# Rotations by a shuffle on VectorE, and compression tokens split by ScalarE and VectorE in three buffers

## What is computed

```python
def rope(x, pos):
    half = ROT_DIM // 2                      # 16
    ...
    x1, x2 = xr[..., :half], xr[..., half:]
    rot = jnp.concatenate([x1 * cos - x2 * sin, x2 * cos + x1 * sin], axis=-1)

def compress(z, pe, w1, w2):                 # once for kc, once for vc
    zb = z[:, blk] + pe[None, None, :, None, :]      # 15 windows of 32 tokens, 16 apart
    zb = zb.transpose(0, 1, 3, 2, 4).reshape(b, n_cmp, NSA_KV_HEADS, CMP_LEN * HEAD_DIM)
    return jax.nn.silu(zb @ w1) @ w2

k_cmp = compress(k_c, cmp_pe[0], cmp_w1[0], cmp_w2[0])
v_cmp = compress(v_c, cmp_pe[1], cmp_w1[1], cmp_w2[1])
k_cmp = rope(k_cmp, positions[:, blk[:, -1]])
```

## Time and profile before

| | |
|---|---|
| median of 3 runs | 2145.42 us (2143.68 to 2145.71) |
| the profiled execution | 2145.21 us, its span 2143.4 us |
| TensorE busy | 2081.5 us, 97% of the span |
| VectorE busy | 1455.8 us, 68% |
| ScalarE busy | 996.9 us, 47% |
| GpSimd busy | 569.5 us, 27% |
| chain that ended last | TensorE 84%, GpSimd 6%, VectorE 5%, ScalarE 2% |
| `ks` to the end of `vw` with both compressions | 454.1 to 590.2 us of the span |

### The profile page before, as it was taken

How to read it: one execution, slowest core, us unless ns; L and a number is a source line. 1 busy time by engine, 2 the same in 40 slices (tenths; PEclk the granted TensorE clock), 3 DMA queues, 4 the chain that set the end, 5 groups by cost and what they waited for, 6 DMA issues and landing times.

```text
span 2143.4 us, 29511 instructions
## 1 busy us (share of the span) xinstructions
PE 2081.5 (97%) x11630; PEld 1770.5 (83%) x11630; DVE 1455.8 (68%) x1984; ACT 996.9 (47%) x1428; POOL 569.5 (27%) x551
## 2 busy tenths in 40 slices
PE   7999999999899999989999999999999999999997
PEld 6788888887788888778877888788888888888886
DVE  8866777677666556667655767677777557777755
ACT  5445444444532545443455554454454335454443
POOL 8205542233400244692121222311110001011122
PEclk9999999999999999999999999999999999999998
DMA  6554665555554433464544445555666665656664
GB/s 248 173 187 149 188 187 188 186 178 188 193 174 140 133 109 117 150 220 149 167 156 145 141 150 164 176 183 183 193 183 182 188 189 186 187 185 189 181 184 135
DMA packets 104090, 370.01 MB, mean 173 GB/s; under 512 B 11632, under 2 KB 12944, under 8 KB 103824
## 3 DMA queue, kind: packets, MB, share of 16 engines
q1 hardware_dynamic: 103952, 368.13, 54.5%
HBM read 365.98 MB, written 2.10 MB: 172 GB/s over the span
## 4 chain that ended last, share of the span: by engine, by line
PE 84%; POOL 6%; DVE 5%; issue 2%; ACT 2%; DMA 0%; SPq 0%; DVEq 0%; POOLq 0%; ACTq 0%
PE psg L508 46%; PE psg L510 22%; POOL s_zf L2357 2%; PE psg L555 2%; DVE s_wl L1579 2%; PE psg L557 2%; PE psg L556 2%; PE psg L507 2%; PE pst L508 1%; ACT s_wh L1064 1%; POOL s_acc L2533 1%; POOL s_psq L2526 1%; POOL s_psq L2281 1%; POOL s_acc L2284 1%; PE pst L592 1%
## 5 line engine op out<-in xcount | busy, mean ns | idle before, releaser
L1579 DVE TENSOR_TENSOR s_wl<-s_stage,s_wh 128x1024 fp32r<-128x1024 f32 (+3 forms) x699 | 869.4, 1245 | 391.8 <-ACT s_wh L1064 389.5
L1064 ACT ACTIVATE s_wh<-s_stage 128x1024 fp32r<-128x1024 f32 (+3 forms) x699 | 725.8, 1041 | 673.7 <-PE psg L508 360.2
L508 PE MATMUL psg<-s_ry,s_wh 128*128 128x512 f32 x2672 | 947.6, 402 | 3.4 <-DVE s_mv L1646 2.5
L510 PE MATMUL psg<-s_ry,s_wl 128*128 128x256 f32 x2501 | 705.0, 282 | 0.0
L508 PEld LDWEIGHTS psg<-s_ry,s_wh 128*128 128x128 f32 x2672 | 494.6, 189 | 121.0 <-issue 8.0
L508 PE MATMUL psg<-s_rh,s_wh 128*128 128x512 f32 x1280 | 462.5, 406 | 18.9 <-DVE s_rh L1597 9.1
L510 PEld LDWEIGHTS psg<-s_ry,s_wl 128*128 128x128 f32 x2501 | 474.4, 190 | 7.2
L510 PE MATMUL psg<-s_rh,s_wl 128*128 128x256 f32 x1180 | 333.0, 282 | 0.0
L508 PEld LDWEIGHTS psg<-s_rh,s_wh 128*128 128x128 f32 x1280 | 238.9, 189 | 78.7 <-issue 13.3
L508 PE MATMUL psg<-s_hid,s_wh 128*128 128x512 f32 x704 | 246.0, 399 | 0.0
L510 PEld LDWEIGHTS psg<-s_rh,s_wl 128*128 128x128 f32 x1180 | 225.1, 191 | 2.8
(11 more groups left out here) (389 smaller groups left out, 2318.2 us busy)
## 6 DMA issues: line engine op xcount, KB each, us to landing
s_stage<-in_wo SPq DMA_DIRECT2D x96, 512.0 KB, 3.6
s_stage<-in_wg SPq DMA_DIRECT2D x88, 512.0 KB, 3.5
s_stage<-in_wu SPq DMA_DIRECT2D x88, 512.0 KB, 3.9
s_stage<-in_ain SPq DMA_DIRECT2D x64, 512.0 KB, 3.5
s_stage<-in_wd SPq DMA_DIRECT2D x64, 448.0 KB, 3.4
s_stage<-in_wkv SPq DMA_DIRECT2D x32, 512.0 KB, 3.6
s_stage<-in_wd SPq DMA_DIRECT2D x32, 512.0 KB, 3.5
s_stage<-in_bq SPq DMA_DIRECT2D x24, 512.0 KB, 3.5
```

The costliest lines, as they stand in the source:

```text
L508: m = e.matmul(o, M.WH[:, r, ws], xx, start=begin, stop=end)
L510: m = e.matmul(o[:, T:2 * T], M.WL[:, r, ws], xh, start=False, stop=False)
L1064: e.activation(M.WH[:, c % NR, 0:n], M.ST[:, c % NS, 0:n], ACT.Copy).then_inc(S["wh"], 1)
L1579: e.tensor_tensor(M.WL[:, c % NR, 0:n], M.ST[:, c % NS, 0:n], M.WH[:, c % NR, 0:n], ALU.subtract).then_inc(S["wl"], 1)
```

## The change

The permutation product leaves TensorE. VectorE exchanges the halves itself with `stream_shuffle` from SBUF to SBUF; then, one tick later, sin and cos products follow in one tick, and one more tick later the sum. The rotation so takes as many ticks as before, has one VectorE instruction more, and no longer uses PSUM bank `o`.

In the compression GpSimd's part and the buffer `ZF` are gone. ScalarE reads the four strided token sets from `KC` or `VC` itself, with `pe` as its bias, and writes the high parts (four instructions in place of one); VectorE computes (Z + pe) - high over the same strided sets (four `scalar_tensor_tensor` in place of one `tensor_tensor`). `ZB` has three buffers, so step m may be written once TensorE has finished step m - 3.

```diff
@@ constants
-for _n, _w in (("ident", 128), ("cm", 128), ("ca", 32), ("c01", 32), ("ipool", 64), ("perm", 32),
+for _n, _w in (("ident", 128), ("cm", 128), ("ca", 32), ("c01", 32), ("ipool", 64),
...
-    put("perm", (a[:, None] == (a[None, :] + 16) % 32).astype(np.float32))
...
+HALVES = [(i + 16) % 32 for i in range(32)]
@@ Memory
-        self.ZF = alloc(l1c, "zf0", [128, 4, 128])
-        self.ZB = [alloc(l1c, f"zb{i}", [128, 2, 4, 128], F32R) for i in range(2)]
+        self.ZB = [alloc(l1c, f"zb{i}", [128, 2, 4, 128], F32R) for i in range(3)]
...
+    def zb(self, m, part, i):
+
+        return self.ZB[m % 3][:, part, i, :].rearrange("p (h n) -> p h n", h=4)[:, :, 0:15]
@@ tensor_program
-    def rope(r, x2, cols):
-        vacant(("o", r % 2))
-        w.wait_ge("l_con", 16)
-        e.matmul(M.PSO[r % 2][0:32, 0:cols], M.con("perm", 32, 32), x2, start=True, stop=True).then_inc(S["rp_mm"], 1)
-        held["o", r % 2] = ("rp_a", r + 1)
-
-    def rope_pair(r, dst, j, last):
-        yield
-        w.wait_ge(*last)
-        rope(r, dst[0:32, j - 1:j + 1, :], 512)
-
...
-                zb = M.ZB[m % 2]
+                zb = M.ZB[m % 3]
...
             if v == 0:
-                w.wait_ge("cmp", 1)
-                rope(3, M.KCMP[0:32, :, 0:15], 60)
                 yield
                 yield
...
             tile((n, j), H, ready("kv"))
-            if j % 2:
-                side.start(rope_pair((0, 1, 2, 4)[2 * r + j // 2], K, j, P.out[n, j]))
...
         tile(("q", j), Y, ready("h1"))
-        if j % 2:
-            side.start(rope_pair(5 + j // 2, M.QN, j, P.out["q", j]))
@@ scalar_program, compress
             def zb(m):
-                w.wait_ge("zf", 8 * v + m + 1)
-                if 8 * v + m >= 2:
-                    w.wait_ge("units", P.zb[8 * v + m - 2])
-                e.activation(M.ZB[m % 2][:, 0, :, :], M.ZF[:, :, :], ACT.Copy).then_inc(S["zbh"], 1)
+                Z = (M.KC, M.VC)[v]
+                w.wait_ge("zz", 3)
+                w.wait_ge(*P.out[("kc", "vc")[v], 3])
+                if m >= 3:
+                    w.wait_ge("units", P.zb[8 * v + m - 3])
+                elif v:
+                    w.wait_ge("units", P.zb[7])
+                for i in range(4):
+                    l = 4 * m + i
+                    x = e.activation(M.zb(m, 0, i), Z[:, :, l:l + 16 * 14 + 1:16], ACT.Identity, bias=M.vec("pe", 32 * v + l))
+                x.then_inc(S["zbh"], 1)
@@ vector_program
-    def rope(r, x2, cos, sin, n, wd, rt):
+    def rope(r, x2, cos, sin, n, wd, rt, made):
+
         rr = rt[:, :, :].rearrange("p a b -> p (a b)")[:, 0:n * wd].rearrange("p (a b) -> p a b", a=n)
-        w.wait_ge("rp_mm", r + 1)
+        w.wait_ge(*made)
         if r and r != 3:
             w.wait_ge("rp_c", 3 if r == 4 else r)
-        e.tensor_tensor(rr, M.PSO[r % 2][0:32, 0:n * wd].rearrange("p (a b) -> p a b", a=n), sin.unsqueeze(1).broadcast_to([32, n, wd]),
-                        ALU.mult).then_inc(S["rp_a"], 1)
-        yield
+        e.stream_shuffle(rr, x2, HALVES).then_inc(S["rp_s"], 1)
+        yield
+        w.wait_ge("rp_s", r + 1)
+        e.tensor_tensor(rr, rr, sin.unsqueeze(1).broadcast_to([32, n, wd]), ALU.mult).then_inc(S["rp_a"], 1)
         e.tensor_tensor(x2, x2, cos.unsqueeze(1).broadcast_to([32, n, wd]), ALU.mult).then_inc(S["rp_b"], 1)
         yield
...
                 w.wait_ge("zbh", 8 * v + m + 1)
-                e.tensor_tensor(M.ZB[m % 2][:, 1, :, :], M.ZF[:, :, :], M.ZB[m % 2][:, 0, :, :].bitcast(F32), ALU.subtract).then_inc(S["zbl"], 1)
+                Z = (M.KC, M.VC)[v]
+                for i in range(4):
+                    l = 4 * m + i
+                    x = e.scalar_tensor_tensor(M.zb(m, 1, i), Z[:, :, l:l + 16 * 14 + 1:16], M.vec("pe", 32 * v + l),
+                                               M.zb(m, 0, i).bitcast(F32), ALU.add, ALU.subtract)
+                x.then_inc(S["zbl"], 1)
@@ pool_program
-    def compress():
...
-    for i in range(2):
+    for i in range(3):
         e.memset(M.ZB[i][:, :, :, :].bitcast(F32), 0.0).then_inc(S["zz"], 1)
-    e.memset(M.ZF[:, :, :], 0.0).then_inc(S["zz"], 1)
-    side.start(compress())
```

More of the change, by code:

```diff
@@ L973, in tensor_program @@
     side.start(compress())
-    for r, (n, K) in enumerate((("ks", M.KS), ("kw", M.KW))):
+    for n in ("ks", "kw"):
         for j in range(4):
             tile((n, j), H, ready("kv"))
-            if j % 2:
-                side.start(rope_pair((0, 1, 2, 4)[2 * r + j // 2], K, j, P.out[n, j]))
     pair("vs", H, ready("kv"))
@@ L1850, in rope, with rope_pair @@
         e.tensor_tensor(x2, x2, rr, ALU.add).then_inc(S["rp_c"], 1)
-    def rope_pair(r, dst, j):
+    def rope_pair(r, dst, j, made):
         yield
-        yield from rope(r, dst[0:32, j - 1:j + 1, :], M.COS[:, :], M.SIN[:, :], 2, T, M.RT)
+        yield from rope(r, dst[0:32, j - 1:j + 1, :], M.COS[:, :], M.SIN[:, :], 2, T, M.RT, made)
     def compress():
@@ L1887, in compress @@
             if v == 0:
-                w.wait_ge("cmp", 1)
-                steps = rope(3, M.KCMP[0:32, :, 0:15], M.COS[:, 31:256:16], M.SIN[:, 31:256:16], 4, 15, M.RTC)
+                steps = rope(3, M.KCMP[0:32, :, 0:15], M.COS[:, 31:256:16], M.SIN[:, 31:256:16], 4, 15, M.RTC, ("cmp", 1))
                 next(steps)
@@ L2124, in vector_program @@
             if j % 2:
-                side.start(rope_pair((0, 1, 2, 4)[2 * r + j // 2], K, j))
+                side.start(rope_pair((0, 1, 2, 4)[2 * r + j // 2], K, j, P.out[n, j]))
     v_pair("vs", M.VS[:, 0, :], 1, "kv_c")
@@ L2136, in vector_program @@
         if j % 2:
-            side.start(rope_pair(5 + j // 2, M.QN, j))
+            side.start(rope_pair(5 + j // 2, M.QN, j, P.out["q", j]))
     w.wait_ge("hct", 2)
```

## The result

The changed kernel takes 2117.54 us, median of four runs (2116.44 to 2117.80), against 2145.19 of the kernel before on the same chip (four runs, 2143.68 to 2145.71): a ratio of 0.9868 with a 95% interval from 0.9856 to 0.9879. The forecast was 2118.3 us in a range from 2116 to 2129.

A forecast was written before the change was run, and what follows sets the result against it. TensorE, busy 97% of the span, was taken as the bound, idling in the compression stretches through GpSimd's loop. 11.6 + 1.2 + 8.45 + 6.62 - 1.0 = 26.9 us off 2145.2 gave 2118.3 us, range 2116 to 2129.

The forecast's parts named there:

- two products: Rotations: permutation products leave TensorE's path, 1.16 us each with refill; ten in all give 11.6 us.
- late splits: Both compression stretches: some weight splits come late on busy VectorE; 1.0 us given back for the 16 units together.
- The units as a measure: Both compression stretches: length beyond tile, value and compression unit times counts as lost, 8.45 us (keys) and 6.62 us (values).
- The loop: Compression: GpSimd's sums through one `ZF` hold up ScalarE's and VectorE's weight splits, hence TensorE; losses 8.45 and 6.62 us.
- z: Compression: VectorE's time for the four strided instructions of a step, taken as 0.85 us against 0.69 for the one.
- The first rival: Keys' stretch: VectorE becomes the bound if strided elements cost more; z = 2.0 gives 2125 us; chance 0.15.
- The shuffle: VectorE's eleven shuffles of 32 x 512: taken as 0.67 us each, beside TensorE's work, the wait at the scores staying covered.
- The compressed keys: After the product with `cmp_w2`: TensorE's wait for VectorE's copy and the permutation product go, 1.21 us.
- DMA: Both compression stretches: same bytes at about 225 GB/s, hidden until a load's landing takes over 6.2 us.
- The second: Compression stretches: staging slots become the bound, landings of 7 us costing 6 us, 2124 us; chance 0.10.
- the third: Compression stretches: the ring of weight splits, not GpSimd's loop, sets the pace; only 11.6 + 1.2 won, 2132 us; chance 0.07.
- The fourth: Compression: the strided instructions cost VectorE what they cost GpSimd, 4.36 us a step; slower, 2163 us; chance 0.03.

The follow-up runs named there:

- experiment 4: Kernel before with rotations by shuffles, the permutation's constant kept in place, GpSimd keeping the sums with two `ZF` and two `ZB`: 2125.1 us.
- experiment 10: Kernel before with rotations by shuffles, the permutation's constant kept in place, GpSimd keeping the sums with one `ZF` and three `ZB`: 2137.8 us.
- experiment 6: Changed kernel with two token buffers `ZB` in place of three: 2128.38 us.
- Experiment 12: Changed kernel with each of the eleven shuffles issued twice, the extra one into a buffer nothing reads at that time: 2117.65 us.
- experiment 3: Changed kernel with the 32 columns of the permutation's constant kept unused, so what lies behind stays in its place in SBUF: 2120.41 us.
- experiment 8: Changed kernel with 16 unused columns (64 bytes) in place of the 32 of the permutation's constant: 2122.55 us.
- experiment 11: Changed kernel with two waits shortened by reordering on VectorE and ScalarE, and 240 unused columns (960 bytes) behind the constants: 2117.01 us.
- experiment 5: Changed kernel with VectorE's four low-part instructions issued twice, the second set into columns of `ZB` no result uses: 2124.31 us.
- experiment 2: Kernel before with only the compression changed (ScalarE and VectorE, three buffers), permutation products staying on TensorE, constant in place: 2129.36 us.
- experiment 9: Kernel before with rotations by shuffles, the permutation's constant kept in place, GpSimd keeping the sums with two `ZF` and three `ZB`: 2121.5 us.

## Why the prediction was right, and where only its sum was

Step by step, against the profiled executions:

| stretch | forecast | won |
|---|---|---|
| start of the keys' stretch | 0 | -0.15 |
| keys' stretch: 8.45, two products, less late splits | 10.3 | 10.54 |
| from there to the values' compression: two products, 1.21 | 3.5 | 2.13 |
| values' units: 6.62 less late splits | 6.1 | 6.11 |
| from there to the queries | 0 | -0.21 |
| queries: six products | 7.0 | 7.19 |
| up to the scores | 26.9 | 25.6 |
| behind the scores | 0 | +1.8 |

- **The units as a measure** held. The losses of 8.45 and 6.62 us, worked out from unit times instead of idle time, came back as 8.2 and 6.1 us; with 0.5 given back in each for late splits, that is within 0.3 us of the forecast. Idle time alone, 6.2 and 4.5 us, would have given too little.
- **The loop** was rightly read from the chain and the waits, and experiments 4 and 10 show it: a second `ZF` alone opens it. The sentence that then nothing waits for anything but the unit three steps back was right too, but I gave it no price; experiment 6 gives it, 10.8 us. Without the third buffer the forecast would have been far off.
- **z** was 1.00 us and not 0.85: the four strided instructions were mis-sized by 0.15 us, inside the bounds. The instructions of 60 elements take 308 ns each, about 0.25 from start to start, against 0.15 in the earlier trace rows. The first rival's rule, which the Trainium skill (SBUF — State Buffer, The DMA port swizzle) states without a figure, agrees in sign; the new instructions also have an operand per row and round, so the stride alone is not isolated. By the prediction's own formula 0.15 costs nothing, and what the late splits cost (below) stayed under what was given back for them.
- **The shuffle** took 0.72 us against 0.67. The estimate of 0.6 from the Trainium skill (VectorE: DVE Perf Modes, Rules for kernel authors) was lower still. Experiment 12 prices it: two more of them in the keys' part cost 0.6 us, and nine elsewhere nothing.
- **The compressed keys** are the term that failed: 1.21 us were to go, and with the two products of this part 2.13 of 3.53 came. The wait for VectorE's copy had covered another one, which stood behind it: the evacuation of the last `kw` tile, whose bank the first unit of `vs` needs. Before, by the chain in order of time (start us, us, what), that evacuation was done at 524.03 us and the copy at 524.25, both ahead of the first `vs` unit at 524.51:

```profile
522.89 0.70 DVE s_kw L1624
523.61 0.42 DVE s_kw L1631
524.04 0.21 DVE s_kcmp L1885
```

The chain of the changed kernel in order of time (start us, us, what):

```profile
508.58 0.39 ACT s_ht L1232
...
509.00 0.42 DVE s_ht L1880
509.42 0.59 DVE s_rt L1840
510.01 0.60 DVE s_kw L1841
510.61 1.14 DVE s_wl L1572
511.75 0.61 DVE s_kw L1617
...
512.38 0.44 DVE s_kw L1624
...
512.91 0.47 PE psg L558
```

The last matmul of the last `kw` tile starts at 510.97 us. A rotation step and a split stand ahead of its evacuation on VectorE, so that begins at 511.75 and ends at 512.82, and TensorE waits 0.93 us for it. By TensorE's timelines, before and changed, the last matmuls of that tile are these:

```profile
522.45 0.40 PE L508 MATMUL psg<-s_rh,s_wh 128*128 128x512 f32 x1
...
510.97 0.39 PE L511 MATMUL psg<-s_rh,s_wh 128*128 128x512 f32 x1
```

From there to the first unit of `vs` it was 2.06 us (522.45 to 524.51) and is 1.94 now (510.97 to 512.91): of the 1.21 us, 0.1 came. The other 0.3 us that are missing in this part are the slower value units (experiments 3, 8 and 11). The prediction took the wait for the copy as the last one at this place and asked what is late next only for the splits.
- **Late splits** cost 0.4 and 0.5 us in the parts from the first to the eighth compression unit (31.44 - 31.03 and 31.24 - 30.73, with units of 2.81 us for the keys); 1.0 was given back for them. Of the second, 0.2 is again the place of the value units' operands: with the constant in its place the part takes 31.06. **DMA**: at 222 and 230 GB/s ScalarE's splits waited for no load in the two stretches.

**Behind the scores** the time was not touched by the sum, yet 1.8 us more were won in the end, out of two parts of opposite sign. The first is a loss: TensorE's granted clock falls from 1.00 (2.4 GHz) to 0.50 (1.2 GHz) while it works on the 48 small products of the scores, or right behind them. Busy times by stretch, before and changed:

```profile
687.00:688.00 1.00, 1.00 (x8) 0.96 (x8) 0.49 (x2) 0.00 (x0) 0.00 (x0) 0.87 0.72 279
688.00:691.00 3.00, 3.00 (x11) 2.52 (x11) 2.20 (x7) 0.60 (x2) 0.00 (x0) 0.50 0.02 7
691.00:692.00 1.00, 1.00 (x7) 0.88 (x7) 0.97 (x6) 0.00 (x0) 0.00 (x0) 0.93 0.04 8
```

```profile
660.00:661.00 1.00, 1.00 (x9) 1.00 (x8) 0.00 (x0) 0.00 (x0) 0.00 (x0) 0.74 0.86 205
661.00:667.00 6.00, 6.00 (x23) 5.42 (x23) 3.15 (x10) 0.60 (x2) 0.00 (x0) 0.50 0.25 79
667.00:668.00 1.00, 1.00 (x7) 0.82 (x6) 0.97 (x7) 0.00 (x0) 0.00 (x0) 0.85 0.00 0
```

Counting the shares of the border slices, it is down for 3.4 us before and for 6.8 now, which costs 1.7 us more at half speed. The twelve heads behind them take 10.10 us each in place of 10.05, 0.6 together; with the constant in its place they take 10.05 again, so this part is the place in SBUF. Where the heads end, the gain is 23.3. The second is a win: from there on it grows to 27.4, in the long stretches of plain units by 0.033 us with each pair, by the places in SBUF (experiment 3). Against the kernel with the constant in its place the change itself is worth 24.8 us by the medians. So the forecast of 2118.3 against 2117.5 owes part of its closeness to luck, to a term it did not have: the mechanism and the sizes of the loop were right, and 1.3 us too much at the keys and 2.3 us lost behind the scores were made good by 4.1 us that nobody had planned.

Of the rivals, the first holds at z = 2.0, as experiment 5 shows, and not at 1.0. The second and the third are excluded by the waits and by experiments 2 and 4. The fourth needed 0.8 us an instruction on VectorE, and each takes 0.31.

## What to carry to other kernels

Where an engine that works in order waits for a buffer, look at what stands behind the waiting instruction, and try one more buffer before moving the work: here the second `ZF` and the third `ZB` were worth 15.6 of the 17.2 us that the two parts lost to the loop in the kernel with the rotations changed, and moving the additions off GpSimd itself 1.6, which the times cannot tell from nothing. Count the loss of a stretch in units of known length and not in idle time, and ask of every wait that goes which other one it was covering. A small time difference over a whole program can come from the place of an operand; keep the places when a term of a few microseconds is to be judged, and judge it by the part of the trace where it lies.

## What was not expected of the hardware

- 128 bytes of place in SBUF changed every plain tile unit by 0.6% (5.653 and 5.620 us a pair), some 4 us from the heads to the end, and made the value units and the heads slower; the rule stays open.
- The fall of TensorE's clock to 1.2 GHz at the scores lasts for very different times in kernels that do the same there: 3.4 us before, 6.8 in the changed kernel, 10.2 in the one with the constant in its place (experiment 3):

```profile
655.00:657.00 2.00, 2.00 (x21) 2.00 (x20) 1.97 (x4) 1.06 (x1) 0.00 (x0) 1.00 0.73 250
658.00:668.00 10.00, 10.00 (x39) 9.13 (x39) 4.14 (x16) 0.73 (x3) 0.00 (x0) 0.50 0.21 73
```

  These scores began at 654.9 us, and the clock fell within 3 us; before the change it fell only when they were done. In the profiled executions of the others it is down for 3.4 us in experiments 6 and 9, for 10.2 in 2, and for 6.8 in the rest. Up to 3.4 us of a comparison of such kernels are thus decided at this place, and what sets the length was not tried.
- GpSimd's additions of 60 elements took 972 ns each in the mean in the kernel before, beside VectorE's 308 for more work on the same elements. That mean mixes two kinds: by the instructions of `s_zf` from 440 to 590 us (ns min/median/max) and the timelines of GpSimd and VectorE, half of them take 0.49 us or less, and the longest last over VectorE's splits and end 0.3 us after one of them. Of the 4.36 us that the prediction took as GpSimd's price for a step, 3.0 were one such instruction; the lines are of another step of that length:

```profile
L2357 POOL TENSOR_SCALAR s_zf<-s_kc,s_vec x28: 479/485/2996, 461.8 to 496.9; 128x60 f32<-128x60 f32 x28
...
481.54 2.98 POOL L2357 TENSOR_SCALAR s_zf<-s_kc,s_vec 128x60 f32<-128x60 f32 x1
...
481.26 1.27 DVE L1579 TENSOR_TENSOR s_wl<-s_stage,s_wh 128x1024 fp32r<-128x1024 f32 x1 [0.26 <-ACT s_wh L1064]
...
483.05 1.20 DVE L1579 TENSOR_TENSOR s_wl<-s_stage,s_wh 128x1024 fp32r<-128x1024 f32 x1
```
